# Byte addresses of the split operands in the three feed-forwards of a two-block kernel

## The reference, cut to what matters

```
def swiglu(x, w_gate, w_up, w_down):
    return (jax.nn.silu(x @ w_gate) * (x @ w_up)) @ w_down
```

## Time and profile before

| what | value |
|---|---|
| median of 3 executions | 1210.68 us (1209.78 to 1212.91) |
| span of the profiled execution, first to last instruction | 1206.9 us |
| TensorE matmuls | 9128, busy 98% of the span |
| mean granted clock of TensorE | 0.987 |
| matmuls of the three feed-forwards | 4752 |

### The profile page before, as it was taken

The page is one execution under the profiler, slowest core; times in us unless marked ns, Lnnn a source line. Parts: engine busy times, 40 slices in busy tenths (PEclk is TensorE's granted clock), DMA queues, the critical chain, the costliest instruction groups (busy, mean ns, idle before and its releaser), DMA issues.

```text
span 1206.9 us, 24404 instructions
## 1 busy us (share of the span) xinstructions
PE 1178.4 (98%) x9128; PEld 1111.1 (92%) x9128; DVE 816.0 (68%) x1121; ACT 637.3 (53%) x1018; POOL 527.1 (44%) x285
## 2 busy tenths in 40 slices
PE   6999999999999999999999999999999999999998
PEld 6999999987889899999999879987877999999998
DVE  7788875856865577777654852688836596655555
ACT  6444446525762555454546546468517635655553
POOL 0343436732465533343436645458530483232331
PEclk9999998999999999999989999999999999999999
DMA  6888884543334467878614333233323254666663
GB/s 221 277 278 294 283 280 130 190 140 123 105 108 137 157 210 259 292 274 292 188 52 158 123 99 129 88 106 105 105 70 106 88 175 140 208 185 188 188 189 121
DMA packets 58100, 207.10 MB, mean 172 GB/s; under 512 B 6576, under 2 KB 8240, under 8 KB 57776
## 3 DMA queue, kind: packets, MB, share of 16 engines
q1 hardware_dynamic: 49824, 177.23, 45.2%
q0 software_dynamic: 6912, 25.17, 5.7%
q10 hardware_dynamic: 1296, 3.74, 0.9%
HBM read 205.07 MB, written 1.05 MB: 171 GB/s over the span
## 4 chain that ended last, share of the span: by engine, by line
PE 82%; DVE 8%; issue 3%; ACT 3%; POOL 2%; DMA 1%; DVEq 0%; SPq 0%; POOLq 0%; ACTq 0%
PE psum L641 23%; PE psum L642 23%; PE psum L643 22%; POOL own_parts L2944 2%; PE psum L789 1%; PE psum L1017 1%; PE psum L942 1%; PE psum L652 1%; PE psum L654 1%; PE psum L653 1%; PE psum L666 1%; PE psum L1346 1%; POOL high L3039 1%; DVE u_parts L2882 1%; PE psum L700 1%
## 5 line engine op out<-in xcount | busy, mean ns | idle before, releaser
L641 PE MATMUL psum<-parts 128*128 128x256 f32 x1584 | 441.0, 278 | 14.0 <-DVE parts L2197 10.4
L642 PE MATMUL psum<-parts 128*128 128x256 f32 x1584 | 445.7, 281 | 0.0
L643 PE MATMUL psum<-parts 128*128 128x256 f32 x1584 | 441.6, 279 | 0.0
L641 PEld LDWEIGHTS psum<-parts 128*128 128x128 f32 x1584 | 299.5, 189 | 14.9 <-issue 11.0
L2952 POOL TENSOR_TENSOR parts<-low,parts 128x1024 fp32r<-128x1024 f32 x60 | 151.0, 2517 | 367.4 <-ACT parts L1520 367.4
L643 PEld LDWEIGHTS psum<-parts 128*128 128x128 f32 x1584 | 299.7, 189 | 0.0
L642 PEld LDWEIGHTS psum<-parts 128*128 128x128 f32 x1584 | 299.7, 189 | 0.0
L1520 ACT ACTIVATE parts<-low 128x1024 fp32r<-128x1024 f32 x198 | 207.4, 1056 | 163.1 <-DMA low<-stream 162.4
L2944 POOL TENSOR_TENSOR own_parts<-low,parts 128x1024 fp32r<-128x1024 f32 x75 | 184.9, 2479 | 151.5 <-ACT parts L1598 147.4
L2197 DVE TENSOR_TENSOR parts<-low,parts 128x1024 fp32r<-128x1024 f32 x138 | 163.6, 1219 | 23.6 <-ACT parts L1520 22.9
L642 PE MATMUL psum<-u_parts,parts 128*128 128x256 f32 (+1 forms) x560 | 164.7, 294 | 0.0
(11 more groups left out here) (384 smaller groups left out, 2091.1 us busy)
## 6 DMA issues: line engine op xcount, KB each, us to landing
low<-stream SPq DMA_DIRECT2D x334, 512.0 KB, 3.6
high<-conditioning POOLq DMA_DIRECT2D x48, 512.0 KB, 5.0
high<-wuq ACTq DMA_DIRECT2D x1, 1152.0 KB, 5.1
low<-x SPq DMA_DIRECT2D x4, 256.0 KB, 6.3
high<-ctx ACTq DMA_DIRECT2D x1, 1024.0 KB, 6.4
out<-low SPq DMA_DIRECT2D x8, 128.0 KB, 1.8
low<-cst ACTq DMA_DIRECT2D x1, 850.5 KB, 4.8
low<-vec ACTq DMA_DIRECT2D x1, 157.5 KB, 6.3
```

Of the source, the lines that this page charges most:

```text
L641: pe.matmul(out, w_hi[:, cols_], x_hi, start=start, stop=False, **kw)
L642: pe.matmul(out, w_hi[:, cols_], x_lo, start=False, stop=False, **kw)
L643: return pe.matmul(out, w_lo[:, cols_], x_hi, start=False, stop=stop, **kw)
```

## The change

The table `PART_STARTS` with its three columns for k = 0, 1, 2 goes; one table `PART_START` takes its place for all three. `ring_lo` gets no offset, the lower parts of input and hidden values get the same offset as the upper parts, 48 words, and the first chunk of the input's lower part (`AHEAD = 1`) stays 32 words in front of the rest, at 16 words. No instruction is added, removed or moved on any engine; only addresses change. The diff, cut where lines only lose their index `[k]`:

```diff
-PART_STARTS = ({"ring_lo": 16, "u_hi": 112, "u_lo": 16, "hidden_hi": 112, "hidden_lo": 144},
-               {"ring_lo": 16, "u_hi": 112, "u_lo": 80, "hidden_hi": 112, "hidden_lo": 144},
-               {"ring_lo": 16, "u_hi": 112, "u_lo": 80, "hidden_hi": 112, "hidden_lo": 208})
+AHEAD = 1
+PART_START = {"u_lo": 48, "u_hi": 48, "hidden_hi": 48, "hidden_lo": 48}
...
         def ffn_parts(name, n, width):
 
-            return [parts[:, PARTS[name][0] + starts.get(name, 0):PARTS[name][0] + starts.get(name, 0) + n * width]
-                    .rearrange("p (a b) -> p a b", a=n) for starts in PART_STARTS]
-
-        ring_hi = parts[:, 0:RING * TILE].rearrange("p (a b) -> p a b", a=RING)
-        ring_lo = ffn_parts("ring_lo", RING, TILE)
+            at = PARTS[name][0] + PART_START.get(name, 0)
+            return parts[:, at:at + n * width].rearrange("p (a b) -> p a b", a=n)
+
+        ring_hi, ring_lo = ffn_parts("ring_hi", RING, TILE), ffn_parts("ring_lo", RING, TILE)
         u_hi, u_lo = ffn_parts("u_hi", DC, T), ffn_parts("u_lo", DC, T)
+        u_lo = [parts[:, PARTS["u_lo"][0] + 16 + n * T:PARTS["u_lo"][0] + 16 + (n + 1) * T] for n in range(AHEAD)] \
+            + [u_lo[:, n, :] for n in range(AHEAD, DC)]
         hidden_hi, hidden_lo = ffn_parts("hidden_hi", 2, T), ffn_parts("hidden_lo", 2, T)
...
-                return ring_hi[:, j % RING, :], ring_lo[k][:, j % RING, :]
+                return ring_hi[:, j % RING, :], ring_lo[:, j % RING, :]
...
-                                               (u_hi[k][:, c_, :], u_lo[k][:, c_, :]),
+                                               (u_hi[:, c_, :], u_lo[c_]),
```

More of the change, by code:

```diff
@@ L732, in gate_up_first @@
                             mm = split_product(half_bank(PJ[0], a), split_tile(k, a), slice(c_ * P, (c_ + 1) * P),
-                                               (u_hi[k][:, c_, :], u_lo[k][:, c_, :]), c_ == 0 and a == 0, c_ == DC - 1,
+                                               (u_hi[:, c_, :], u_lo[c_]), c_ == 0 and a == 0, c_ == DC - 1,
                                                skip_group_check=True)
@@ L742, in down @@
                         mm = split_product(acc[n], w, slice(n * P, (n + 1) * P),
-                                           (hidden_hi[k][:, par, :], hidden_lo[k][:, par, :]),
+                                           (hidden_hi[:, par, :], hidden_lo[:, par, :]),
                                            first and n % 2 == 0, last, skip_group_check=True)
@@ L1505, in input_upper @@
             def input_upper(k, n, g):
-                act.activation(u_hi[k][:, n, :], h[:, n, :], ACT.Identity, scale=v(g, n)).then_inc(S("input_upper"), 1)
+                act.activation(u_hi[:, n, :], h[:, n, :], ACT.Identity, scale=v(g, n)).then_inc(S("input_upper"), 1)
             def uppers(k, first, last):
@@ L1525, in upper_hidden @@
                 act.wait_ge(S("hidden_ready"), count + 1)
-                act.activation(hidden_hi[k][:, par, :], hidden[:, par, :], ACT.Copy)\
+                act.activation(hidden_hi[:, par, :], hidden[:, par, :], ACT.Copy)\
                    .then_inc(S("hidden_upper"), 1)
@@ L2113, in _ @@
                 act.wait_ge(S("prescaled"), 16 + n + 1)
-                act.activation(u_hi[2][:, n, :], u1[:, n, :], ACT.Identity, bias=modc[:, 24 + n, 0:1])\
+                act.activation(u_hi[:, n, :], u1[:, n, :], ACT.Identity, bias=modc[:, 24 + n, 0:1])\
                    .then_inc(S("input_upper"), 1)
@@ L2196, in lower @@
                 dve.wait_ge(S("upper_ready"), more * RING + (3 * FC * k + j + 1))
-                dve.tensor_tensor(ring_lo[k][:, j % RING, :], ring[:, t % RING, :], ring_hi[:, j % RING, :],
+                dve.tensor_tensor(ring_lo[:, j % RING, :], ring[:, t % RING, :], ring_hi[:, j % RING, :],
                                   ALU.subtract).then_inc(S("lower_ready"), 1)
@@ L2202, in lower_hidden @@
                 dve.wait_ge(S("hidden_upper"), count + 1)
-                dve.tensor_tensor(hidden_lo[k][:, par, :], hidden[:, par, :], hidden_hi[k][:, par, :],
+                dve.tensor_tensor(hidden_lo[:, par, :], hidden[:, par, :], hidden_hi[:, par, :],
                                   ALU.subtract).then_inc(S("hidden_split"), 1)
@@ L2208, in lower_input @@
                 dve.wait_ge(S("input_upper"), DC * k + n + 1)
-                dve.scalar_tensor_tensor(out=u_lo[k][:, n, :], in0=h[:, n, :], scalar=v(g, n), in1=u_hi[k][:, n, :],
+                dve.scalar_tensor_tensor(out=u_lo[n], in0=h[:, n, :], scalar=v(g, n), in1=u_hi[:, n, :],
                                          op0=ALU.mult, op1=ALU.subtract).then_inc(S("input_split"), 1)
@@ L2214, in lower_shifted @@
                 dve.wait_ge(S("input_upper"), DC * 2 + n + 1)
-                dve.scalar_tensor_tensor(out=u_lo[2][:, n, :], in0=u1[:, n, :], scalar=modc[:, 24 + n, 0:1],
-                                         in1=u_hi[2][:, n, :], op0=ALU.add, op1=ALU.subtract)\
+                dve.scalar_tensor_tensor(out=u_lo[n], in0=u1[:, n, :], scalar=modc[:, 24 + n, 0:1],
+                                         in1=u_hi[:, n, :], op0=ALU.add, op1=ALU.subtract)\
                    .then_inc(S("input_split"), 1)
@@ L2951, in lower @@
                 pool.wait_ge(S("upper_ready"), more * RING + (3 * FC * k + j + 1))
-                pool.tensor_tensor(ring_lo[k][:, j % RING, :], ring[:, t % RING, :], ring_hi[:, j % RING, :],
+                pool.tensor_tensor(ring_lo[:, j % RING, :], ring[:, t % RING, :], ring_hi[:, j % RING, :],
                                    ALU.subtract).then_inc(S("lower_ready_2"), 1)
```

## The result

The changed kernel is slower: median 1215.58 us (1214.06 to 1220.35, 20 executions) against 1209.96 us (1203.52 to 1216.33, 20 executions) of the kernel before; ratio 1.0057, 95% interval 1.0043 to 1.0071. The time lies inside the stated range, at its upper end, but the sign is the wrong one: this is the rival "it locks into the slow rhythm", to which 0.23 was given.

A forecast was written before the change was run, and what follows sets the result against it. TensorE's matmul pitch was taken to bound the feed-forwards; 6.2 ns saved per triple x 1452 triples gave 9.0 us, so 1210.7 - 9.0 = 1201.7 us, with 1199 to 1216 us for 8 in 10.

The forecast's parts named there:

- it locks into the slow rhythm: Rival: whole stream of each feed-forward at 118.1 ns per matmul, +11.0 to +12.0 us, 1221 to 1223 us; chance 0.23.
- Part 1: Feed-forward matmuls outside the first input chunk: with L641's residues 0 and 64 they take its pitch, 341.1 ns a triple.
- Part 2: Equal residues, read off the branch merge: the stream locks into one of two rhythms, 113.6 or 118.1 ns, until disturbed.
- Part 3: First chunk's lower part at 128: 132 triples unchanged, 0 us; its disturbance breaks a slow lock at gate or up tiles.
- part 5: Everything between the feed-forwards: untouched, 0 us.
- Part 4: ACT, DVE and POOL in the feed-forwards: other addresses, 0 or few ns, hidden; DVE's 146.7 us of 184 still covered.

The follow-up runs named there:

- Experiment 3: Kernel before, all activations from 0, upper weights from 64, lower weights from 128, 192, 0 in feed-forwards one to three: 118.2, 113.3, 122.3 ns per matmul.
- experiment 10: Changed kernel run again without edit for a second profile: feed-forwards of 189.8, 189.8 and 186.9 us.
- Experiment 11: Changed kernel with the first chunk's lower part from 192 modulo 256 instead of 128: median 1201.77 us, ratio 0.9967 to the kernel before.
- experiment 2: Kernel before, weights from 64; lower activations, by feed-forward, from 0, from 128 in the input alone, from 128 everywhere: partly 113.3, fast and slow tiles, 117.9 ns.
- experiment 6: Changed kernel with AHEAD = 0, the first chunk's lower part at 0 like all others: median 1210.60 us, ratio 1.0021 to the kernel before.
- Experiment 9: Kernel before with all activations from 0, upper weights from 64, lower weights from 192, profiled a second time: span 1206.9 us, one timed execution 1208.57 us.
- experiment 1: Kernel before, both weight parts from 64, all activations from 64, 192, 128 in feed-forwards one to three: 120.0, 118.7, 117.9 ns per matmul.
- experiment 4: Kernel before, weights from 64; lower activations from 64, then 192, upper from 0; third feed-forward upper from 128, lower from 0: 119.3, 119.2, 117.8 ns.
- experiment 5: Kernel before with all activations from 0, upper weights from 64, lower weights from 192 in all three feed-forwards: median 1203.65 us, ratio 0.9942.

## Why the prediction was wrong

- **What bounds the kernel:** right. The feed-forwards hang on TensorE's pitch alone, and addresses change it: from 113.3 to 122.3 ns over these runs with nothing else changed. The Trainium skill, page "TensorE: Matmul & The Clock Gate", section "Part 2: What happens when you issue a matmul", gives TensorE two independent read ports, so that the load of the next weights doesn't slow the running matmul. From that I had worked out that addresses would cost nothing; the measurement decides against it. Whether the ports are the place where the time is lost, no run here shows.
- **Part 1, "the pitch follows L641's":** wrong as it was put. Experiment 3 shows that the pair of addresses in a matmul doesn't set its price.
- **Part 2, two rhythms:** right, and a good guess from little: the fast one was read off one run of eleven matmuls. 113.6 and 118.1 were read, 113.3 and 117.8 measured.
- **Part 3 is the step that failed.** I counted the odd chunk as a kick that frees the stream from the slow rhythm, by likeness to L642 before. It does the opposite: it throws a fast stream into the slow rhythm each time, eight times of eight (experiment 10), and never frees a slow one. I had no row of that pair, took the most favourable reading of a bound that went both ways, and put 0.57 on it. Experiment 11 shows that a kick from 192 does what I had hoped for: 1201.77 us. But part 3 is not all of it. Without the chunk (experiments 2 and 6) the feed-forwards are only partly fast, and the median is 1210.60 us, no gain: the residues 0 and 64 alone, on which the sum rested, don't keep a stream in the good rhythm.
- **The slow rival's size:** 11 to 12 us were foretold; 8.9 us in the feed-forwards, since 117.8 is less than 118.1 and the first five tiles of each feed-forward are partly slow-clocked, waiting or still fast; and 3.2 of it came back in the stretch after feed-forward 2, which part 5 had put at 0, by the granted clock as far as the profiles show. So it was luck that the time fell into the stated range: the full slow lock, which came, had been left out of it, at 1221 to 1223.
- **Part 4:** the cover by DVE was misjudged. Experiment 9: 146.7 us busy of 184 isn't free if a DVE instruction stands still behind POOL's and the hidden part waits behind both.

## What to carry to other kernels

Where matmuls and weight loads stream back to back, look at the pitch (stretch over records) and at whether the lines of a repeating group are alike; if a short run and a long run of the same code have two pitches, the arrangement has two rhythms, and the question is what sets it back, not what the fast one costs. An arrangement in which one operand of the group has another residue can be steady and fast (lower weights from 192: 113.3 ns) or steady and slow (from 0: 122.3), so sweep the residues of each operand apart, one arrangement for each phase of the program, and repeat the profile of the winner before believing it.

## What the runs showed of the hardware that was not expected

- With addresses as the only difference, back-to-back pairs of a 128x128 load and a 128x256 float32r matmul have steady pitches of 113.3, 115.6, 117.8, 118.2, 118.7, 118.9, 119.3, 120.0 and 122.3 ns at the full clock. In spells at 0.5 of it the arrangement doesn't show: at the start of feed-forward 2 the pitch is 213 or 214 ns in the kernel before, the changed kernel and experiments 1, 3, 4 and 5 alike.
- A stream with both parts of each operand at one residue stays in the rhythm in which it is for hundreds of matmuls, and a pause of a tenth of a microsecond can change it.
- The same 400 us after feed-forward 2 are not the same in each kernel: within 5 us of its end the granted clock fell to 0.5 for 6.8 us in eight of the 18 profiles (three of three of the kernel before), for 3.4 us in two, and not at all in eight (two of two of the changed kernel).
- A DVE subtraction of 128x1024 that takes 1.22 us took 3.41 or 3.42 when it started behind a running one of POOL, and ended 1.1 us after it, six times in one feed-forward (experiment 9).
